# Four branches of the second block in three reduced-precision products, begun inside the last attention round

## The chip, the cores and the metric

One of the eight cores of a Trainium2 chip runs the kernel. The metric is the device time of one execution in microseconds (us), median over the executions. TensorE (PE) multiplies matrices, ScalarE (ACT) applies functions and copies, VectorE (DVE) does elementwise work, SyncE (SP) issues the transfers from HBM. TensorE writes to PSUM, which has 8 banks.

## What is computed

Two transformer blocks of width 1,024 on 256 tokens, in fp32. The first has two layers (a convolution and gating mixer with a feed-forward part, then latent attention with eight experts). The second block, which the change touches, is, cut to its mixer:

```python
h = rms_norm(x, norm_mix)
qa, ka, va, u, qm, km, vm, gates = split_in(h @ w_in)
ya = swa_attention(qa, ka, va, sinks, slopes_swa) @ w_o_swa      # 512 -> 1024
z  = gelu(s5_ssm(u, ...)) @ w_glu                                # 512 -> 1024
yb = (z[..., :512] * sigmoid(z[..., 512:])) @ w_o_ssm            # 512 -> 1024
yc = moba_attention(qm, km, vm, slopes_moba) @ w_o_moba          # 512 -> 1024
g = sigmoid(gates)
mixed = g[..., :1024] * ya + g[..., 1024:2048] * yb + g[..., 2048:] * yc
x = x + mixed @ w_out
```

and a feed-forward part (1,024 to 4,096 and back) follows. The products with w_o_swa, w_glu, w_o_moba and w_o_ssm are the four branches.

## The kernel before

Each engine has its own program, written out by hand; semaphores order them, and no scheduler moves anything. Activations lie transposed, features on the partitions and 256 tokens along the columns. Weights come from HBM in chunks of 2 MB into `ring`, which has 3 places: chunk n goes to place n % 3, and SyncE issues it once the chunk three before is used up. In the second block the chunks are numbered `C2_A`, `C2_B`, `C2_QA`, ... `C2_SWA` (10) to `C2_SSM` (13), then `C2_OUT`, `C2_FF1`, `C2_FF2`.

**Attention rounds.** A loop `for r in range(ROUNDS + 1)` with ROUNDS = 8 runs the state-space scan of round r beside the two attention heads of round r - 1, and between them TensorE does the projections that are left (24 tiles of gates). A head a goes through `scores` (TensorE, L1428 and L1429), `biased` (VectorE, L2644 on), `soft` (ScalarE, L1912), `normalised` (VectorE, L2661 to L2664), `turn2` (three transposes on TensorE, L1436), `take_turned` (ScalarE, L1922) and `values` (TensorE). There is one PSUM bank for the transposed probabilities. In the last turn, r = 8, neither scan nor projection is left: only the last output of the scan (`state_output`, its gelu on ScalarE at L1938) and heads 14 and 15. ScalarE's copy of their result (L1954) ends the round.

**Branches.** Each branch has 8 tiles of 128 output features; a tile is 4 matmuls of 256 columns (`group`, L915) in one bank, from bank g % 8. Before a tile with g of 8 or more TensorE waits until VectorE has emptied tile g - 8 (`s_br_free`). VectorE multiplies each tile by its gate and adds it to `mixed` (first branch L2685, later L2690 and L2692); for w_glu ScalarE takes the sigmoid of one tile (L1959), and VectorE multiplies it by the next (L2699). The order is w_o_swa, w_o_moba, w_glu, w_o_ssm. Then the output projection multiplies `mixed` by w_out, 8 tiles of 8 matmuls, also by `group`.

**Matmuls here.** `group` multiplies plain fp32 operands; the trace shows two records for each of its matmuls. `product` (L922 to L924) splits both operands in a high part, copied to fp32r by ScalarE, and a low part, the difference, made by VectorE, and sums high x high, high x low, low x high: three matmuls of one record each. The feed-forward part of the second block already uses `product`; a weight unit there is 128 partitions x 1,024 numbers, split by one ScalarE copy (L1961) and one VectorE subtraction (L2712).

## Time and profile before

| | us |
|---|---|
| median of 3 runs | 2283.11 |
| lowest and highest | 2281.93, 2283.22 |
| the profiled execution, its own time | 2281.74 |
| its span, first to last instruction | 2280.0 |

The profile is of one execution. Its times are counted from the span's start. Its own time is 1.74 us above the span and 1.37 us below the median of the runs. "Idle before" a row, in brackets, is how long the engine stood still ahead of it, with what ended the wait. The end of a matmul is modelled; the distance from one start to the next is what an unbroken stream of them costs. A matmul's record in a timeline can stand for many (x192), so that a row's length is that of the group.

### The profile page before, as it was taken

What the parts mean: (1) busy time and instruction counts of PE and PEld (TensorE: products, weight loads), DVE (VectorE), ACT (ScalarE), POOL (GpSimd) and SP (SyncE); (2) the same over time, 40 slices, a digit from 0 to 9 for tenths busy, and PEclk for the clock granted to TensorE, in tenths of its full rate; (3) what the DMA queues carried; (4) which work ended last, traced back from release to release, by engine and by line L of the source; (5) the groups of instructions that cost most, each with busy time, mean ns of one, the idle gap of its engine ahead of it and who ended that gap; (6) DMA issues with size and microseconds to landing.
All of it is one profiled execution on the core that took longest, in us unless ns stands there. A gap on an engine that the chain in (4) does not pass through costs nothing.

```text
span 2280.0 us, 35361 instructions
## 1 busy us (share of the span) xinstructions
PE 2141.0 (94%) x14994; PEld 1323.6 (58%) x14994; DVE 827.5 (36%) x1568; ACT 518.9 (23%) x965; POOL 56.8 (2%) x93
## 2 busy tenths in 40 slices
PE   5998899999978989998899999999999999899997
PEld 2566688888844573432323343343333878788997
DVE  4798522234532442132001200200123366525554
ACT  4124322234421421001000100000001143303443
POOL 0000000000014000000000000000002000000000
PEclk8999999999999989999989999999999999999999
DMA  9884233222212139999999999999996323144541
GB/s 375 332 349 168 75 110 106 79 101 102 85 44 111 56 136 378 362 378 404 416 413 394 375 398 384 391 361 400 412 398 233 111 76 110 74 148 167 180 174 52
DMA packets 160307, 536.69 MB, mean 235 GB/s; under 512 B 7072, under 2 KB 31776, under 8 KB 139168
## 3 DMA queue, kind: packets, MB, share of 16 engines
q1 hardware_dynamic: 160016, 534.08, 61.7%
q8 instruction: 108, 1.77, 0.3%
q0 software_dynamic: 144, 0.52, 0.1%
q14 instruction: 39, 0.32, 0.0%
HBM read 533.53 MB, written 1.05 MB: 234 GB/s over the span
## 4 chain that ended last, share of the span: by engine, by line
PE 81%; DVE 8%; DMA 6%; DVEq 3%; issue 1%; ACT 1%; SPq 0%; ACTq 0%
PE psum L915 15%; PE psum L1302 15%; PE psum L922 9%; PE psum L923 9%; PE psum L924 9%; PE psum L1306 6%; PE psum L1327 6%; DMA ring<-in_o_exp_w 4%; PE psum L1331 3%; DVE region L2160 2%; DVEq L2163 1%; PE psum L939 1%; DMA region<-in_o_exp_w 1%; PE psum L1235 1%; DVE rstd L2023 1%
## 5 line engine op out<-in xcount | busy, mean ns | idle before, releaser
L922 PE MATMUL psum<-region_r 128*128 128x512 f32 (+1 forms) x1232 | 434.6, 353 | 25.6 <-DVE region_r L2252 8.7
L923 PE MATMUL psum<-region_r 128*128 128x512 f32 (+1 forms) x1136 | 392.2, 345 | 0.0
L924 PE MATMUL psum<-region_r 128*128 128x512 f32 (+1 forms) x1136 | 390.5, 344 | 0.0
L922 PEld LDWEIGHTS psum<-region_r 128*128 128x128 f32 x1232 | 236.9, 192 | 69.7 <-issue 31.9
L924 PEld LDWEIGHTS psum<-region_r 128*128 128x128 f32 x1136 | 217.8, 192 | 25.3
L923 PEld LDWEIGHTS psum<-region_r 128*128 128x128 f32 x1136 | 218.0, 192 | 24.8
L1302 PE MATMUL psum<-ring,region 128*32 128x512 f32 (+1 forms) x1792 | 183.4, 542 | 2.3 <-DMA ring<-in_o_exp_w 2.3
L915 PE MATMUL psum<-H,ring 128*128 128x256 f32 (+1 forms) x656 | 156.3, 396 | 6.1 <-ACT H L1615 6.1
L1302 PE MATMUL psum<-region 128*32 128x512 f32 (+1 forms) x1520 | 153.3, 535 | 2.5 <-DMA region<-in_o_exp_w 1.5
L915 PE MATMUL psum<-region,ring 128*128 128x256 f32 (+1 forms) x592 | 139.1, 396 | 12.2 <-DVE region L2301 9.6
L915 PEld LDWEIGHTS psum<-H,ring 128*128 128x128 f32 x656 | 124.5, 192 | 34.5 <-issue 16.2
L915 PEld LDWEIGHTS psum<-region,ring 128*128 128x128 f32 x592 | 113.0, 192 | 38.0 <-issue 20.6
L1302 PEld LDWEIGHTS psum<-ring,region 128*32 128x32 f32 x1792 | 56.5, 110 | 112.2 <-issue 97.4
L2485 DVE COPY rstd<-psum 128x512 f32<-128x512 f32 x6 | 4.2, 692 | 292.7 <-PE psum L1331 260.8
L1831 ACT ACTIVATE region<-psum 128x256 f32<-128x256 f32 (+2 forms) x56 | 24.8, 450 | 373.7 <-PE psum L1259 280.3
L2498 DVE COPY region<-psum 64x512 f32<-64x512 f32 (+1 forms) x56 | 35.1, 626 | 186.8 <-PE psum L1306 186.1
L1302 PEld LDWEIGHTS psum<-region 128*32 128x32 f32 x1520 | 48.2, 110 | 91.1 <-issue 78.7
L1306 PE MATMUL psum<-ring,region 128*32 128x512 f32 (+1 forms) x832 | 98.4, 564 | 2.7 <-DMA ring<-in_o_exp_w 2.7
L2535 DVE TENSOR_TENSOR region<-region,psum 128x512 f32<-128x512 f32 (+1 forms) x28 | 17.0, 620 | 227.1 <-PE psum L1306 183.9
L1306 PE MATMUL psum<-region 128*32 128x512 f32 (+1 forms) x792 | 87.7, 539 | 5.0 <-DMA region<-in_o_exp_w 4.3
L1327 PE MATMUL psum<-ring,region 128*32 128x512 f32 x736 | 86.2, 594 | 2.2 <-DMA ring<-in_o_exp_w 2.2
L2160 DVE SCALAR_TENSOR_TENSOR region<-region,param 128x512 f32<-128x512 f32 x120 | 84.8, 748 | 4.1 <-issue 0.4
(362 smaller groups left out, 2452.5 us busy)
## 6 DMA issues: line engine op xcount, KB each, us to landing
ring<-in_o_exp_w SPq DMA_DIRECT2D x165, 1024.0 KB, 10.3
region<-in_o_exp_w SPq DMA_DIRECT2D x141, 1024.0 KB, 10.5
ring<-in_w_ada SPq DMA_DIRECT2D x24, 2048.0 KB, 10.3
ring<-in_w_ff SPq DMA_DIRECT2D x16, 2048.0 KB, 8.0
H<-in_o_exp_w SPq DMA_DIRECT2D x30, 1024.0 KB, 10.3
ring<-in_e_ffn_w SPq DMA_DIRECT2D x22, 1024.0 KB, 7.8
ring<-in_w_in SPq DMA_DIRECT2D x10, 2048.0 KB, 8.0
region<-in_e_w_in SPq DMA_DIRECT2D x4, 2048.0 KB, 16.0
```

The lines of the kernel that those rows point to most:

```text
L915: mm = pe.matmul(dst, lhsT, rhs, start=(i == 0), stop=(i == len(pairs) - 1))
L922: pe.matmul(out, a_hi, b_hi, start=first, stop=False)
L923: pe.matmul(out, a_hi, b_lo, start=False, stop=False)
L924: mm = pe.matmul(out, a_lo, b_hi, start=False, stop=last)
L939: mm = pe.matmul(bank(NORM_BANK.get(n, 7))[:, 0:w], ones[:, :], squares[:, tile, 0:w], start=(k == 0), stop=(k == kt - 1))
L1302: mm = pe.matmul(psum[r:r + 32, to, 0:width], x_full[:, k, slot0 + 32 * tg:slot0 + 32 * tg + 32], moving, start=(k == 0), stop=(k == KT - 1))
L1306: mm = pe.matmul(psum[r:r + 32, to, 0:width], x_full[:, k, slot0:slot0 + 32], moving, start=(k < 2), stop=(k >= KT - 2))
L1327: mm = pe.matmul(psum[r:r + 32, grp.down[q], :], he[:, i, slot0 + 32 * tg:slot0 + 32 * tg + 32], moving, start=(i == 0), stop=(i == ET - 1))
L1331: mm = pe.matmul(psum[r:r + 32, grp.down[q], :], he[:, i, slot0:slot0 + 32], moving, start=(i < 2), stop=(i >= ET - 2))
L1831: act.activation(he[:, tiles, slot0:slot0 + w].rearrange("p (b c) w -> p c b w", b=b), bank(grp.turn[p])[:, 0:b * c * w].rearrange("p (c b ...
L2160: x = dve.scalar_tensor_tensor(conv[i], apad[:, i, :, k:k + T], taps[:, i, k:k + 1], conv[i], ALU.mult, ALU.add)
L2498: dve.tensor_copy(cross_sum[0:64, to, 0:width], psum[64:128, b, 0:width])
```

## The change

The four branches are computed with `product`. Each branch is cut in four units of two tiles; ScalarE copies a unit's weights to one of four fp32r buffers (`unit_hi`), VectorE writes the difference over the weights in `ring`, and the same is done once for the 4 x 256 values of each branch (`values_high`, `values_low`; for the last branch tile by tile). w_glu moves ahead of w_o_moba, in TensorE's work and in SyncE's order of transfers. The first two units (tiles 0 to 3) and their splits stand in the last turn of the attention loop; bank numbers are shifted by 4 for it. The output projection stays a plain `group`.

The diff, cut to its core (renamed semaphores are left out: `s_weights_hi` and `s_weights_lo` are the old `s_z_hi` and `s_z_lo`, `s_values_hi` and `s_values_lo` the old `s_bo_hi` and `s_bo_lo`):

```diff
+BRANCHES = (C2_SWA, C2_GLU, C2_MOBA, C2_SSM)
+BRANCH_UNITS = 4 * len(BRANCHES)
+UNITS_BEFORE, VALUES_BEFORE = Z_GROUPS, 4
+B_SPLIT = 4
+EARLY_UNITS = 2
+def branch_bank(g):
+    return (g + 2 * EARLY_UNITS) % 8
+def branch_tiles(u):
+    b, i = divmod(u, 4)
+    return (4 + i, i) if BRANCHES[b] == C2_GLU else (2 * i, 2 * i + 1)
...
+        unit_hi = [reg_r(21504 + 1024 * i, 1024) for i in range(B_SPLIT)]
+        qa_hi, qm_hi = reg_r(25600, 4, T), reg_r(26624, 4, T)
+        u_hi, glu_hi = reg_r(12288, 4, T), reg_r(13312, 4, T)
+        qa_lo, qm_lo, u_lo, glu_lo = reg_r(6144, 4, T), reg_r(7936, 4, T), reg_r(9728, 4, T), reg_r(19968, 4, T)
+        branch_values = [(qa, qa_hi, qa_lo), (u_T, u_hi, u_lo), (qm, qm_hi, qm_lo), (glu_z, glu_hi, glu_lo)]
...
-            for n, w in ((C2_SWA, "w_o_swa_2"), (C2_MOBA, "w_o_moba_2"), (C2_GLU, "w_glu_2"), (C2_SSM, "w_o_ssm_2")):
+            for n, w in ((C2_SWA, "w_o_swa_2"), (C2_GLU, "w_glu_2"), (C2_MOBA, "w_o_moba_2"), (C2_SSM, "w_o_ssm_2")):
...
+            def branch(b, units):
+                _, hi, lo = branch_values[b]
+                for u in (4 * b + i for i in units):
+                    pe.wait_ge(s_weights_lo, UNITS_BEFORE + u + 1)
+                    w, v = branch_hi(u), branch_unit(u, ring_r)
+                    for i, tile in enumerate(branch_tiles(u)):
+                        g = 2 * u + i
+                        if g >= 8:
+                            pe.wait_ge(s_br_free, g - 7)
+                        h = int(tile >= 4) if BRANCHES[b] == C2_GLU else i
+                        for k in range(4):
+                            if u == 4 * b and i == 0:
+                                pe.wait_ge(s_values_lo, VALUES_BEFORE + 4 * b + k + 1)
+                            mm = product(bank(branch_bank(g))[:, 0:T], [(w[:, k, h, :], v[:, k, h, :], hi[:, k, :], lo[:, k, :])], k == 0, k == 3)
+                        mm.then_inc(s_br_ready, 1)
...
+                if r == ROUNDS:
+                    pe.wait_ge(s_proj_sb, len(PROJ))
+                    pe.wait_ge(s_xs_used, ROUNDS)
+                    branch(0, range(EARLY_UNITS))
...
-            pe.wait_ge(s_proj_sb, len(PROJ))
             pe.wait_ge(s_ao_sb, 8)
             pe.wait_ge(s_y_sb, 4)
-            pe.wait_ge(s_xs_used, ROUNDS)
-            branch(C2_SWA, 0, qa, range(8))
-            branch(C2_MOBA, 8, qm, range(8))
-            branch(C2_GLU, 16, u_T, (4, 0, 5, 1, 6, 2, 7, 3))
-            pe.wait_ge(s_br_free, 24)
-            branch(C2_SSM, 24, glu_z, range(8))
+            branch(0, range(EARLY_UNITS, 4))
+            for b in range(1, len(BRANCHES)):
+                branch(b, range(4))
...
+            def unit_high(u):
+                n = BRANCHES[u // 4]
+                if u % 4 == 0:
+                    act.wait_ge(w_in[n % RING], landed2(n))
+                if u == 0:
+                    act.wait_ge(s_xs_ready, ROUNDS)
+                last = u - B_SPLIT
+                if last >= 0:
+                    act.wait_ge(s_br_ready, 2 * last + 2)
+                act.activation(branch_hi(u), branch_unit(u), ACT.Copy).then_inc(s_weights_hi, 1)
+            def values_high(b):
+                v, hi, _ = branch_values[b]
+                act.activation(hi, v, ACT.Copy).then_inc(s_values_hi, 4)
...
+                    act.drain()
+                    values_high(0)
+                    for u in range(EARLY_UNITS):
+                        unit_high(u)
...
+            act.drain()
+            unit_high(EARLY_UNITS)
+            unit_high(EARLY_UNITS + 1)
+            values_high(1)
+            values_high(2)
+            for u in range(EARLY_UNITS + 2, BRANCH_UNITS):
+                unit_high(u)
+                if 6 <= u < 10:
+                    i = u - 6
+                    act.wait_ge(s_br_ready, 8 + 2 * i + 1)
+                    if i >= 2:
+                        act.wait_ge(s_br_free, 8 + 2 * (i - 1))
+                    act.activation(glu_s[:, i % 2, :], bank(branch_bank(8 + 2 * i))[:, 0:T], ACT.Sigmoid).then_inc(s_glu_sig, 1)
+                if 8 <= u < 12:
+                    act.wait_ge(s_br_free, 8 + 2 * (u - 8) + 2)
+                    act.activation(glu_hi[:, u - 8, :], glu_z[:, u - 8, :], ACT.Copy).then_inc(s_values_hi, 1)
...
+            def unit_low(u):
+                dve.wait_ge(s_weights_hi, UNITS_BEFORE + u + 1)
+                dve.tensor_tensor(branch_unit(u, ring_r), branch_unit(u), branch_hi(u).bitcast(F32), ALU.subtract).then_inc(s_weights_lo, 1)
+            def values_low(b):
+                v, hi, lo = branch_values[b]
+                dve.wait_ge(s_values_hi, VALUES_BEFORE + 4 * b + 4)
+                dve.tensor_tensor(lo, v, hi.bitcast(F32), ALU.subtract).then_inc(s_values_lo, 4)
...
+                    values_low(0)
+                    for u in range(EARLY_UNITS):
+                        unit_low(u)
...
+            unit_low(EARLY_UNITS)
+            unit_low(EARLY_UNITS + 1)
+            dve.wait_ge(s_proj_sb, len(PROJ))
+            values_low(1)
+            for u in range(BRANCH_UNITS):
+                b, i = divmod(u, 4)
+                if EARLY_UNITS + 2 <= u + 2 < BRANCH_UNITS:
+                    unit_low(u + 2)
+                if u == 4:
+                    values_low(2)
+                if b == 2:
+                    dve.wait_ge(s_values_hi, VALUES_BEFORE + 12 + i + 1)
+                    dve.tensor_tensor(glu_lo[:, i, :], glu_z[:, i, :], glu_hi[:, i, :].bitcast(F32), ALU.subtract).then_inc(s_values_lo, 1)
+                if b == 0:
+                    for g in (2 * u, 2 * u + 1):
+                        dve.wait_ge(s_br_ready, g + 1)
+                        dve.tensor_tensor(mixed[:, g, :], bank(branch_bank(g))[:, 0:T], gates[:, g, :], ALU.mult).then_inc(s_br_free, 1)
+                if b == 1:
+                    dve.wait_ge(s_glu_sig, i + 1)
+                    dve.wait_ge(s_br_ready, 8 + 2 * i + 2)
+                    dve.tensor_tensor(glu_z[:, i, :], bank(branch_bank(9 + 2 * i))[:, 0:T], glu_s[:, i % 2, :], ALU.mult).then_inc(s_br_free, 2)
+                if b >= 2:
+                    for g in (2 * u, 2 * u + 1):
+                        add_branch(g, 16 if b == 2 else 8)
```

How the rows of each engine's program move, at three places (line numbers of before are those of the profile; after the change `group` is L950, `product` L957 to L959, the scores L1463 and L1464, the transposes L1471).

TensorE at the end of the last attention round, in the kernel before; `region,ring` rows are the branches, and brackets name the semaphores that a row waits for:

```order
L1429 MATMUL psum<-region 128x256
L1436 MATMUL psum<-const,region 128x128 [waits apt_sb,ap_ready]
L1436 MATMUL psum<-const,region 128x128 x2
L1436 MATMUL psum<-const,region 128x128 [waits apt_sb,ap_ready]
L1436 MATMUL psum<-const,region 128x128 x2
L915 MATMUL psum<-region 64x128 [waits y_sb,ao_sb,apt_sb]
L915 MATMUL psum<-region 64x128 x2
L915 MATMUL psum<-region 64x128 [waits apt_sb]
L915 MATMUL psum<-region 64x128 x2
L915 MATMUL psum<-region,ring 128x256 [waits xs_used,y_sb,w_in1,ao_sb,proj_sb]
```

The same place after the change, where the semaphores of the splits go by their program names z_lo and bo_lo:

```order
L1464 MATMUL psum<-region 128x256
L957 MATMUL psum<-region_r 128x256 [waits z_lo,bo_lo,xs_used,proj_sb]
L958 MATMUL psum<-region_r 128x256
L959 MATMUL psum<-region_r,ring_r 128x256
...
L1471 MATMUL psum<-const,region 128x128 [waits apt_sb,ap_ready]
...
L950 MATMUL psum<-region 64x128 [waits apt_sb]
L950 MATMUL psum<-region 64x128 x2
L957 MATMUL psum<-region_r 128x256 [waits z_lo,y_sb,ao_sb]
```

48 matmuls of tiles 0 to 3 now stand between the last scores and the first transpose; the other 28 tiles stand behind the last values, as before.

ScalarE from the last turn of the loop on, after the change (L2017 ends a round's heads, L1980 and L1975 are copies of values and of weight units, L2001 is the gelu, L1953 the exponentials, L1963 the copy of transposed probabilities):

```order
L2017 ACTIVATE region<-psum 128x256 [waits ao_ready]
L1980 ACTIVATE region_r<-region 128x1024
L1975 ACTIVATE region_r<-ring 128x1024 [waits xs_ready,w_in1]
L1975 ACTIVATE region_r<-ring 128x1024
L2001 ACT_TABLE_LOAD
L2001 ACTIVATE region<-psum 128x256 [waits y_psum]
...
L1963 ACTIVATE region<-psum 128x384 [waits ao_ready,apt_ready] x2
L2017 ACTIVATE region<-psum 128x256 [waits ao_ready]
L1975 ACTIVATE region_r<-ring 128x1024 x2
L1980 ACTIVATE region_r<-region 128x1024 x2
L1975 ACTIVATE region_r<-ring 128x1024 [waits br_ready,w_in2]
```

Before the change the gelu and its table load followed the first of these rows at once. Three copies of 1,024 columns now stand ahead of it, and the copies of the third and fourth unit stand behind the round's last copy.

VectorE in the third branch after the change (L2743 is the subtraction for a weight unit, L2790 that for a tile of the gated values, L2774 and L2776 take a tile into `mixed`):

```order
L2743 TENSOR_TENSOR ring_r<-ring,region_r 128x4x256 [waits z_hi]
L2790 TENSOR_TENSOR region_r<-region,region_r 128x256 [waits bo_hi]
L2774 TENSOR_TENSOR region<-psum,region 128x256 [waits br_ready]
L2776 TENSOR_TENSOR region<-region 128x256
L2774 TENSOR_TENSOR region<-psum,region 128x256 [waits br_ready]
L2776 TENSOR_TENSOR region<-region 128x256
```

Before, a tile was taken into `mixed` by two rows of the same kind (L2690 and L2692), and nothing else stood there: the first two of these rows are new for every two tiles.

## Rows read from the trace of the kernel before

**Rows 1.** The page: the span, and the chain that ended last by line.

```profile
span 2280.0 us, 35361 instructions
...
PE psum L915 15%; PE psum L1302 15%; PE psum L922 9%; PE psum L923 9%; PE psum L924 9%; PE psum L1306 6%; PE psum L1327 6%; DMA ring<-in_o_exp_w 4%; PE psum L1331 3%; DVE region L2160 2%; DVEq L2163 1%; PE psum L939 1%; DMA region<-in_o_exp_w 1%; PE psum L1235 1%; DVE rstd L2023 1%
```

**Rows 2.** Timeline of TensorE, end of attention to out-projection: start, us, line, operation, count.

```profile
1966.88 0.49 PE L1436 MATMUL psum<-const,region 128*128 128x128 f32 x3
...
1973.76 0.61 PE L1429 MATMUL psum<-region 64*128 64x256 f32 x4
1978.05 0.90 PE L1436 MATMUL psum<-const,region 128*128 128x128 f32 x3 [3.68 <-DVE region L2664]
1979.62 0.87 PE L1436 MATMUL psum<-const,region 128*128 128x128 f32 x3 [0.67 <-ACT region L1922]
...
1983.13 42.38 PE L915 MATMUL psum<-region,ring 128*128 128x256 f32 x192 [0.52 <-issue]
2026.13 14.08 PE L915 MATMUL psum<-region,ring 128*128 128x256 f32 x64 [0.62 <-DVE region L2699]
2041.23 3.94 PE L915 MATMUL psum<-region,ring 128*128 128x256 f32 x17 [1.02 <-DVE region L2692]
```

**Rows 3.** Timeline of TensorE in the first feed-forward product, at either clock.

```profile
2075.59 0.41 PE L922 MATMUL psum<-region_r 128*128 128x256 f32 x1
2075.80 0.41 PE L923 MATMUL psum<-region_r 128*128 128x256 f32 x1
...
2095.23 0.28 PE L922 MATMUL psum<-region_r 128*128 128x256 f32 x1
2095.35 0.28 PE L923 MATMUL psum<-region_r 128*128 128x256 f32 x1
```

**Rows 4.** Timeline of ScalarE around the last attention round.

```profile
1968.85 0.38 ACT L1954 ACTIVATE region<-psum 128x256 f32<-128x256 f32 x1 [0.96 <-PE psum L915]
1969.26 1.28 ACT L1938 ACT_TABLE_LOAD   x1
1973.54 0.38 ACT L1938 ACTIVATE region<-psum 128x256 f32<-128x256 f32 x1 [3.00 <-PE psum L915]
```

**Rows 5.** Timeline of VectorE: last attention round, then one tile of the second branch.

```profile
1974.39 0.55 DVE L2644 SCALAR_TENSOR_TENSOR region<-const,psum 128x384 f32<-128x384 f32 x1 [6.17 <-PE psum L1429]
...
1978.80 0.35 DVE L2664 TENSOR_SCALAR region<-region,small 128x256 f32<-128x256 f32 x1
...
1999.65 0.42 DVE L2690 TENSOR_TENSOR region<-psum,region 128x256 f32<-128x256 f32 x1 [1.30 <-PE psum L915]
2000.15 0.43 DVE L2692 TENSOR_TENSOR region<-region 128x256 f32<-128x256 f32 x1
```

**Rows 6.** Groups of ScalarE by form in the feed-forward stage: us, mean ns.

```profile
L1961 ACT ACTIVATE region_r<-ring 128x1024 fp32r<-128x1024 f32 x31 | 31.2, 1060 | 0.0
```

**Rows 7.** Timeline of VectorE: a subtraction of 1,024 columns and what follows.

```profile
2076.05 1.22 DVE L2712 TENSOR_TENSOR region_r<-ring,region_r 128x1024 fp32r<-128x1024 f32 x1
2077.18 0.48 DVE L2027 SCALAR_TENSOR_TENSOR H<-X,param,rstd 128x256 f32<-128x256 f32 x1
```

**Rows 8.** Timeline of TensorE: a short gap in the first mixer.

```profile
181.01 2.52 PE L1009 MATMUL psum<-region,ones 128*128 128x512 f32 x4 [1.94 <-DVE region L2160]
```

**Rows 9.** Windows: busy us per engine, then clock, DMA share, GB/s.

```profile
182.00:183.00 1.00, 1.00 (x4) 0.50 (x2) 1.00 (x3) 0.00 (x0) 0.00 (x0) 0.66 1.05 410
...
185.00:186.00 1.00, 1.00 (x4) 0.84 (x3) 0.66 (x3) 0.96 (x3) 0.00 (x0) 0.63 0.11 41
...
1977.00:1978.00 1.00, 0.00 (x0) 0.00 (x0) 0.84 (x5) 0.67 (x3) 0.00 (x0) 0.87 0.00 0
...
1984.00:1985.00 1.00, 1.00 (x5) 0.77 (x5) 0.00 (x0) 0.34 (x1) 0.00 (x0) 0.72 0.09 16
```

**Rows 10.** DMA of the fourth branch's weights: its issue, and us to landing.

```profile
1997.92 0.37 SPq L870 DMA_DIRECT2D ring<-in_w_o_ssm  x1
...
ring<-in_w_o_ssm SPq DMA_DIRECT2D x1, 2048.0 KB, 7.8
```

More of the change, by code:

```diff
@@ L384, in build @@
         s_mh_hi = sem("mh_hi")
-        s_z_hi = sem("z_hi")
-        s_z_lo = sem("z_lo")
+        s_weights_hi = sem("z_hi")
+        s_weights_lo = sem("z_lo")
         s_heads_in = sem("heads_in")
-        s_bo_hi = sem("bo_hi")
-        s_bo_lo = sem("bo_lo")
+        s_values_hi = sem("bo_hi")
+        s_values_lo = sem("bo_lo")
         s_cat_hi = sem("cat_hi")
@@ L729, in out_lo, with branch_unit, branch_hi @@
             return out_unit(q, ring_r)
+        def branch_unit(u, memory=ring):
+            n = BRANCHES[u // 4]
+            v = memory[:, n % RING, :].rearrange("p (k n) -> p k n", k=4)
+            if n == C2_GLU:
+                return v.rearrange("p k (h c) -> p k h c", h=2)[:, :, :, P * (u % 4):P * (u % 4) + P]
+            return v[:, :, 2 * P * (u % 4):2 * P * (u % 4) + 2 * P].rearrange("p k (h c) -> p k h c", h=2)
+        def branch_hi(u):
+            return unit_hi[u % B_SPLIT].rearrange("p (k h c) -> p k h c", k=4, h=2)
         def cols(w, c, n, rows=None):
@@ L1032, in _ @@
                 if q < 2:
-                    pe.wait_ge(s_bo_lo, 2 * kk + 2)
+                    pe.wait_ge(s_values_lo, 2 * kk + 2)
                 if q == 2:
@@ L1484, in _ @@
                     values(2 * r - 1)
-            def branch(n, first, src, order):
-                pe.wait_ge(w_in[n % RING], landed2(n))
-                w = slot(n, 4, D)
-                for i, tile in enumerate(order):
-                    g = first + i
-                    if g >= 8:
-                        pe.wait_ge(s_br_free, g - 7)
-                    group(bank(g % 8)[:, 0:T], [(w[:, k, tile * P:(tile + 1) * P], src[:, k, :]) for k in range(4)]
-                          ).then_inc(s_br_ready, 1)
-            pe.wait_ge(s_proj_sb, len(PROJ))
             pe.wait_ge(s_ao_sb, 8)
             pe.wait_ge(s_y_sb, 4)
-            pe.wait_ge(s_xs_used, ROUNDS)
-            branch(C2_SWA, 0, qa, range(8))
-            branch(C2_MOBA, 8, qm, range(8))
-            branch(C2_GLU, 16, u_T, (4, 0, 5, 1, 6, 2, 7, 3))
-            pe.wait_ge(s_br_free, 24)
-            branch(C2_SSM, 24, glu_z, range(8))
+            branch(0, range(EARLY_UNITS, 4))
+            for b in range(1, len(BRANCHES)):
+                branch(b, range(4))
             pe.wait_ge(s_br_free, 32)
@@ L1653, in weights_hi @@
                     act.wait_ge(s_z_ready, m - 1)
-                act.activation(z_hi(m), z_unit(m), ACT.Copy).then_inc(s_z_hi, 1)
+                act.activation(z_hi(m), z_unit(m), ACT.Copy).then_inc(s_weights_hi, 1)
             weights_hi(0)
@@ L1701, in _ @@
                 act.wait_ge(s_bo_ready, i + 1)
-                act.activation(cat_hi[:, 4 + i, :], u_out[:, i, :], ACT.Copy).then_inc(s_bo_hi, 1)
+                act.activation(cat_hi[:, 4 + i, :], u_out[:, i, :], ACT.Copy).then_inc(s_values_hi, 1)
             act.wait_ge(s_lna_sum, 2)
@@ L1954, in _ @@
                     act.activation(dst[:, (r - 1) % 4, :], bank(3)[:, 0:T], ACT.Copy).then_inc(s_ao_sb, 1)
-            for i in range(4):
-                act.wait_ge(s_br_ready, 16 + 2 * i + 1)
-                if i >= 2:
-                    act.wait_ge(s_br_free, 16 + 2 * (i - 1))
-                act.activation(glu_s[:, i % 2, :], bank((16 + 2 * i) % 8)[:, 0:T], ACT.Sigmoid).then_inc(s_glu_sig, 1)
+            act.drain()
[14 more added lines that the diff above has]
+                    act.activation(glu_hi[:, u - 8, :], glu_z[:, u - 8, :], ACT.Copy).then_inc(s_values_hi, 1)
             def ff1_split(cs, u):
@@ L2669, in _ @@
                     state_drive(r)
+                else:
+                    values_low(0)
+                    for u in range(EARLY_UNITS):
+                        unit_low(u)
                 if r:
@@ L2679, in _ @@
                     state_scan(r, 1)
-            dve.wait_ge(s_proj_sb, len(PROJ))
-            for g in range(8):
-                dve.wait_ge(s_br_ready, g + 1)
-                dve.tensor_tensor(mixed[:, g, :], bank(g)[:, 0:T], gates[:, g, :], ALU.mult).then_inc(s_br_free, 1)
             def add_branch(g, gate0):
```

24 lines of the change are left out of this document (9 added, 15 removed).

## The prediction

> **What bounds the kernel now.** I read the page first, then the timeline of TensorE over the part that changes. By the page TensorE's plain matmuls at L915 hold 15% of the chain that ended last, and the waiting there is small [rows 1]: whatever is saved in TensorE's stream in the branches comes off the end, as long as nothing else takes its place. The timeline shows that stream [rows 2]. After the last scores, whose end is 1974.37, TensorE stands still for 3.68 us until VectorE has normalised head 14, then does the two turns and the values at a slow pace, and begins the branches at 1983.13. They run without a break but for 0.62 us ahead of the fourth (w_glu's last product), and the output projection starts at 2041.23. So the stretch to be changed is 58.1 us, and the 8.8 us before it are mostly waiting. All other stages keep their instructions.
>
> **What a tile costs.** Before: the 64 records of the fourth branch stand for 8 tiles of 4 matmuls and last 14.08 us, less a modelled tail of about 0.3: 13.8 / 8 = 1.73 us a tile, 0.43 a matmul [rows 2]. After: 12 matmuls of `product`. The same form in the feed-forward part, 256 columns, starts every 0.12 us at full clock and every 0.21 at half clock [rows 3], so 1.44 us a tile or 2.55. That is 0.29 us less a tile at full clock.
>
> The FP8 and Floating Point Precision page of the Trainium skill (TensorE Precision Notes) says that true fp32 takes four passes through the array, of which `product` makes three. By the page a tile would fall by a quarter, to 1.30 us, and 28 tiles would save 12.0 us where the rows give 8.1. The 0.12 us of the rows decides the sum: the page's version stands below as a rival.
>
> **The last round.** ScalarE ends the seventh round's heads at 1968.85 + 0.38 = 1969.23 [rows 4]. New there: one copy of values and two of weight units, 1.06 us each by the feed-forward rows [rows 6], so until about 1972.4. The gelu's table load (1.28 us) followed at 1969.26 and now follows at 1972.4; it ends at 1973.7, while the gelu began at 1973.54 when TensorE had finished its input [rows 4]. That is 0.15 us late, and nothing waits for it so soon. VectorE was idle for 6.17 us before 1974.39 [rows 5]. Its three subtractions take 1.13 us each from start to start [rows 7], the first one behind ScalarE's first copy at 1970.4: they end at about 1974.0, 0.4 ahead of the softmax work of head 14. So both engines hide their early splits, and units 0 and 1 are ready when TensorE has sent off the scores at 1974.3. Without this cover each microsecond would still be free up to about 1 us, since the softmax ends (1978.80 + 0.35 = 1979.15 [rows 5]) before TensorE is through with the early tiles.
>
> TensorE then runs 48 matmuls x 0.12 = 5.76 us, to 1980.1. The idle 3.68 us are filled and 2.05 us are pushed behind. First turn to second turn took 1.57 us at half clock [rows 2]; at full clock, with a copy of about 0.5 us between them, I take 1.1: the second turn at 1981.2. In round seven, at full clock, ScalarE's closing copy began 1.97 us after the second turn (1966.88 to 1968.85 [rows 2, 4]) and took 0.38: 1983.55.
>
> **The new wait.** Only behind that copy does ScalarE begin with unit 2, and VectorE subtracts only when the copy is made: 0.1 + 1.06 + 1.22 + 0.05 = 2.4 us [rows 6, 7]. TensorE has nothing else queued behind it and stands still from about 1983.15 to 1986.0. That is 2.9 us later than the branches started before, with 28 tiles to go instead of 32.
>
> **The rest of the branches.** 28 x 1.44 = 40.3 us, to 2026.3. Can the splits keep up? A unit is 2.88 us of TensorE. ScalarE has 1.06 us a unit and at most 0.8 more. VectorE has 1.13, plus 0.84 in the first branch and 0.42 in the second; in the third 1.13 + 0.42 for the gated values + 2 x 0.93 (0.50 from multiply to add, then 0.43 [rows 5]) = 3.41, half a microsecond over. It lags, but it subtracts two units ahead. I followed it through: counted from the start of the third branch its last low part of gated values is there at 12.3 us, and TensorE wants it at 4 x 2.88 + 3 x 0.36 = 12.6. So nothing waits, by 0.3 us. If each of its four waits a unit costs 0.1 us more, 1.6 us over the branch, TensorE stands for up to 1.3 us: the upper end of this cost, 0 the lower, and I take 0. The fourth branch needs only 2.99 a unit, and no weights for its last two. The 0.62 us of wait between w_glu and w_o_ssm goes, as the third branch lies between them now. Weights: w_o_ssm is issued when the first branch is done, about 1992 instead of 1997.92, lands 7.8 us later [rows 10] and is copied after 2006; the others land as early, counted from their use. Four PSUM banks lie between a tile and its emptying, as before.
>
> **The clock.** After an idle stretch TensorE is granted half its clock. Here it fell at 1977.7 and rose at 1984.6 (worked out from 0.87 and 0.72 as the means of these two windows [rows 9]), so before the change the end of the round and 1.4 us of the branches ran slow. A gap of just 1.94 us, until 181.01, was followed by a fall at 182.3, and the clock came back at 185.7 [rows 8, 9]. With its early tiles TensorE keeps its clock through the turns, but the new gap of 2.9 us is longer than that one, so I expect a fall about when unit 2 begins. The two slow stretches lasted 3.4 and 6.8 us; a microsecond of them loses 1 - 0.12 / 0.213 = 0.44 us. That is 1.5 us for the short one, about 2.5 for the long one without what of it lies in the gap (3.0 with it), 0 if the clock stays: I take 1.8.
>
> The page TensorE: Matmul & The Clock Gate of the Trainium skill (Why this matters for your kernels) advises against gaps between bursts of matmuls for this reason. [...]
>
> **The sum.** 2026.3 + 0.16 (modelled tail) + 1.02 (the same wait for the last tile of `mixed` [rows 2]) + 1.8 = 2029.3 instead of 2041.2: 11.9 us less. Made up of 8.1 for 28 cheaper tiles, 6.9 for four tiles gone from the stretch, 0.6 for the wait, 0.6 for slow clock at the old start, less 2.9 and 1.8; the remainder is rounding. The profiled execution took 2281.74, so it gives 2269.8. That execution lies 1.4 under the median of the runs, 2283.11, from which it gives 2271.2; I forecast 2270.8. A change of 0.2% (4.6 us) is about what this measurement can tell.
>
> **The rivals.**
> - *The clock stays up*: no fall follows the gap. For it: in both stretches the fall came 3.3 us after the idle time began (at 1974.37 and about 179.07), and here work is back after 2.9. Against it: so it was in the second stretch, after 1.94. 13.7 us less, 2269.0 (15%).
> - *Clock and splits both worse*: the long slow stretch, and VectorE up to 1.3 us late in the third branch. 9.5 us less, 2273.5 (8%).
> - *Three quarters of a plain tile*: a matmul of `product` at a quarter of the plain one's 0.43 us, 0.108, which saves 3.9 us more in 28 tiles and 0.6 in the early ones. 2266.3. Against it: 0.12 in the feed-forward part [rows 3] (2%). This is the rule of the Trainium skill's FP8 and Floating Point Precision page cited above.
> - *It does not act*: weights or values late by so much that the saving is eaten, within 4.6 us of before. Needs 7.3 us of new waits, half a microsecond a unit; no row shows that (2%).
> - *Slower*: the split chain goes in step with TensorE. If a unit's copy and subtraction (2.4 us with their waits) came behind the unit before it instead of beside it, 14 units would cost 33 us: 2304. It decides from 0.85 us of wait a unit, where the 11.9 us are gone. Against it: four buffers for the high parts, and units are subtracted two ahead (3%).
>
> The likeliest case, 70%, has 2269 to 2273 as its own range. The range for 8 in 10 is 2267.5 to 2274.5, which takes in the first two rivals and the 1.4 us between profile and runs. Faster by over 0.2%: 95%. Within 0.2%: 2%. Slower: 3%.
>
> **What would show it.** In the profile after: 48 `product` matmuls from about 1974.3, without a gap before the first turn at 1980.1; a gap of 2.5 to 3.3 us ahead of unit 2, released by VectorE's subtraction; the granted clock 1.0 until then and half for 3 to 6 us after; matmuls 0.12 us apart from there to about 2028; no wait of over 0.3 us in the third and fourth branch. It is wrong if matmuls with low weights in `ring` stand further apart, if the clock stays low, or if VectorE releases TensorE again and again.

## The result and the profile after

| | before | after |
|---|---|---|
| median of 5 runs, us | 2281.93 | 2267.50 |
| lowest and highest | 2280.16, 2283.22 | 2262.80, 2271.60 |
| the profiled execution, its own time | 2281.74 | 2262.80 |
| its span | 2280.0 | 2261.0 |

The ratio is 0.9934 [0.9920, 0.9948], so 12 to 18 us faster; the forecast had 95% on faster. The forecast of 2270.8 was reckoned from a median of 2283.11 over 3 runs; over 5 runs the median of before is 2281.93, 1.2 us lower. From median to median the change gave 14.4 us where 12.3 were forecast. The page of the changed kernel, span and chain, answers to [rows 1]:

```profile
span 2261.0 us, 35681 instructions
...
PE psum L1337 15%; PE psum L950 12%; PE psum L957 10%; PE psum L958 10%; PE psum L959 10%; PE psum L1341 7%; PE psum L1362 6%; DMA ring<-in_o_exp_w 4%; PE psum L1366 3%; DVE region L2234 2%; DVEq L2237 1%; PE psum L974 1%; DMA region<-in_o_exp_w 1%; PE psum L1270 1%; DVE rstd L2097 1%
```

The 15% that the plain matmuls of `group` held are now split: L950 (`group`) 12%, and 10% for each line of `product`, where the branches join the feed-forward part.

TensorE's timeline over the stretch that changed, which answers to [rows 2]:

```profile
1968.33 0.61 PE L1464 MATMUL psum<-region 64*128 64x256 f32 x4
1968.87 0.38 PE L957 MATMUL psum<-region_r 128*128 128x256 f32 x1
...
1974.54 0.28 PE L959 MATMUL psum<-region_r,ring_r 128*128 128x256 f32 x1
1974.66 0.49 PE L1471 MATMUL psum<-const,region 128*128 128x128 f32 x3
1975.83 0.52 PE L1471 MATMUL psum<-const,region 128*128 128x128 f32 x3 [0.67 <-ACT region L1963]
1976.27 1.52 PE L950 MATMUL psum<-region 128*64 128x128 f32 x12
1980.76 0.36 PE L957 MATMUL psum<-region_r 128*128 128x256 f32 x1 [2.96 <-DVE ring_r L2743]
...
1989.83 0.28 PE L958 MATMUL psum<-region_r 128*128 128x256 f32 x1
1989.95 0.28 PE L959 MATMUL psum<-region_r,ring_r 128*128 128x256 f32 x1
...
2020.47 0.28 PE L959 MATMUL psum<-region_r,ring_r 128*128 128x256 f32 x1
2022.12 2.21 PE L950 MATMUL psum<-region,ring 128*128 128x256 f32 x9 [1.37 <-DVE region L2776]
```

Behind the scores 48 matmuls of `product` follow without a break, then the first turn at 1974.66 and the second 1.17 us later. Behind head 15's values TensorE waits 2.96 us, and VectorE's subtraction of a weight unit (L2743) ends it. From 1980.76 on it never waits until the output projection, ahead of which it stands 1.37 us for the last tile of `mixed`.

Two things lie in the 19.0 us between the spans. I take two marks. The first is ScalarE's copy that ends the heads of round seven; up to it the engines run the same instructions in both programs; only the transfers of w_glu and w_o_moba, 2 MB each, come in exchanged order. The second is VectorE's first update of X behind the output projection. "The stretch" below is the time from the first mark to the second. ScalarE's timeline of after, for the first mark and for [rows 4]:

```profile
1963.43 0.38 ACT L2017 ACTIVATE region<-psum 128x256 f32<-128x256 f32 x1 [0.96 <-PE psum L950]
1963.89 1.06 ACT L1980 ACTIVATE region_r<-region 128x1024 fp32r<-128x1024 f32 x1
1964.85 1.99 ACT L1975 ACTIVATE region_r<-ring 128x1024 fp32r<-128x1024 f32 x2
1966.86 1.28 ACT L2001 ACT_TABLE_LOAD   x1
1968.15 0.38 ACT L2001 ACTIVATE region<-psum 128x256 f32<-128x256 f32 x1
...
1977.83 0.38 ACT L2017 ACTIVATE region<-psum 128x256 f32<-128x256 f32 x1 [0.96 <-PE psum L950]
1978.30 2.00 ACT L1975 ACTIVATE region_r<-ring 128x1024 fp32r<-128x1024 f32 x2
```

And VectorE's, which answers to [rows 5] and holds the second mark:

```profile
1966.19 2.35 DVE L2743 TENSOR_TENSOR ring_r<-ring,region_r 128x1024 fp32r<-128x1024 f32 x2
1968.96 0.55 DVE L2718 SCALAR_TENSOR_TENSOR region<-const,psum 128x384 f32<-128x384 f32 x1 [0.42 <-PE psum L1464]
...
1979.38 2.36 DVE L2743 TENSOR_TENSOR ring_r<-ring,region_r 128x1024 fp32r<-128x1024 f32 x2 [5.66 <-ACT region_r L1975]
...
2001.76 1.22 DVE L2743 TENSOR_TENSOR ring_r<-ring,region_r 128x1024 fp32r<-128x1024 f32 x1
...
2004.90 1.22 DVE L2743 TENSOR_TENSOR ring_r<-ring,region_r 128x1024 fp32r<-128x1024 f32 x1
...
2020.79 0.42 DVE L2774 TENSOR_TENSOR region<-psum,region 128x256 f32<-128x256 f32 x1 [0.49 <-PE psum L959]
2021.64 0.42 DVE L2776 TENSOR_TENSOR region<-region 128x256 f32<-128x256 f32 x1 [0.43 <-issue]
2025.88 0.42 DVE L2805 TENSOR_TENSOR X<-X,psum 128x256 f32<-128x256 f32 x1 [3.81 <-PE psum L950]
```

The second mark in the profile of before:

```profile
2044.99 0.42 DVE L2705 TENSOR_TENSOR X<-X,psum 128x256 f32<-128x256 f32 x1 [3.81 <-PE psum L915]
```

The first mark stands at 1963.43, and in the profile of before at 1968.85 [rows 4]: 5.4 us ahead of the change. The first two experiments show that profiles of one and the same kernel differ there by as much. From mark to mark it was 76.14 us before and is 62.45 now: in these two profiles **13.7 us lie where the change is**. Behind the second mark both take 235 us.

| in the stretch | before | forecast | after |
|---|---|---|---|
| first mark to the end of the scores | 5.5 | 5.5 | 5.4 |
| early tiles | - | 5.8 | 5.8 |
| from there to the branches or unit 2 | 8.8 | 5.9 | 6.1 |
| branches, to the output projection | 58.1 | 43.3 | 41.4 |
| to the second mark | 3.8 | 3.8 | 3.8 |

The forecast's 43.3 are 40.3 + 0.16 + 1.02 + 1.8. Its last summand, 1.8 us for a fall of the clock, is where it is off: this profile has nothing of it. The windows of after (busy us of PE, PEld, DVE, ACT, POOL, then granted clock, DMA share, GB/s) have no fall behind the gap, against [rows 9]:

```profile
1980.00:1981.00 1.00, 0.24 (x2) 0.27 (x3) 1.00 (x2) 1.00 (x2) 0.00 (x0) 1.00 0.00 0
1981.00:1982.00 1.00, 1.00 (x10) 1.00 (x10) 1.00 (x2) 1.00 (x2) 0.00 (x0) 1.00 0.00 0
```

### The profile page after: what moved, and what is told of

It reads as the page before. It is cut to its first block, busy times and chain, and to the rows that moved or that the text cites. A ratio compares the mean times of both kernels' runs of the same rounds, so it can differ in the third digit from the quotient of the medians.

```text
span 2261.0 us, 35681 instructions
## 1 busy us (share of the span) xinstructions
PE 2122.1 (94%) x15122; PEld 1317.5 (58%) x15122; DVE 848.6 (38%) x1591; ACT 539.2 (24%) x988; POOL 56.9 (3%) x93
## 4 chain that ended last, share of the span: by engine, by line
PE 81%; DVE 7%; DMA 7%; DVEq 3%; issue 1%; ACT 1%; SPq 0%; ACTq 0%
PE psum L1337 15%; PE psum L950 12%; PE psum L957 10%; PE psum L958 10%; PE psum L959 10%; PE psum L1341 7%; PE psum L1362 6%; DMA ring<-in_o_exp_w 4%; PE psum L1366 3%; DVE region L2234 2%; DVEq L2237 1%; PE psum L974 1%; DMA region<-in_o_exp_w 1%; PE psum L1270 1%; DVE rstd L2097 1%
## 5 line engine op out<-in xcount | busy, mean ns | idle before, releaser
L957 PE MATMUL psum<-region_r 128*128 128x512 f32 (+1 forms) x1360 | 469.6, 345 | 29.5 <-DVE region_r L2326 8.8
L958 PE MATMUL psum<-region_r 128*128 128x512 f32 (+1 forms) x1264 | 427.3, 338 | 0.0
L959 PE MATMUL psum<-region_r 128*128 128x512 f32 (+1 forms) x1136 | 390.3, 344 | 0.0
L957 PEld LDWEIGHTS psum<-region_r 128*128 128x128 f32 x1360 | 260.2, 191 | 74.0 <-issue 36.3
L958 PEld LDWEIGHTS psum<-region_r 128*128 128x128 f32 x1264 | 242.2, 192 | 24.7
L959 PEld LDWEIGHTS psum<-region_r 128*128 128x128 f32 x1136 | 217.7, 192 | 25.0
L950 PE MATMUL psum<-H,ring 128*128 128x256 f32 (+1 forms) x656 | 156.2, 396 | 6.1 <-ACT H L1656 6.1
L950 PEld LDWEIGHTS psum<-H,ring 128*128 128x128 f32 x656 | 124.4, 192 | 34.4 <-issue 16.2
L950 PE MATMUL psum<-region,ring 128*128 128x256 f32 (+1 forms) x336 | 82.6, 406 | 11.4 <-DVE region L2375 9.6
L1362 PE MATMUL psum<-region 128*32 128x512 f32 x688 | 83.4, 614 | 2.8 <-issue 1.6
```

The lines of the kernel that those rows point to most:

```text
L950: mm = pe.matmul(dst, lhsT, rhs, start=(i == 0), stop=(i == len(pairs) - 1))
L957: pe.matmul(out, a_hi, b_hi, start=first, stop=False)
L958: pe.matmul(out, a_hi, b_lo, start=False, stop=False)
L959: mm = pe.matmul(out, a_lo, b_hi, start=False, stop=last)
L1362: mm = pe.matmul(psum[r:r + 32, grp.down[q], :], he[:, i, slot0 + 32 * tg:slot0 + 32 * tg + 32], moving, start=(i == 0), stop=(i == ET - 1))
```

## The experiments

Each gives the stretch from its profile, which leaves out what scatters ahead of the first mark, and the ratio to the kernel before where it was run more than once. "Slow clock" is the time of the stretch at half clock, summed over windows of 1 us as (1 - granted clock) x 2. Each stretch is of one profile, and in the changed kernel the clock alone moves it by up to 2.6 us.

### The kernel before, once more

No edit. It asks what the clock and the stretch of one and the same kernel do from one execution to the next.

> The kernel before, once more, as a kernel of its own. In the two profiles so far the last attention round's closing copy stands at 1968.85 (before) and 1963.43 us (after), though nothing ahead of it was changed. Theory A, chance from one execution to the next: this profile's copy stands anywhere within 1962 to 1970 us, the times of the runs spread over some 3 to 9 us, and the ratio to before is 1.000 within 0.002. Rival B, the changed kernel really runs 5 us faster ahead of the branches: this profile's copy stands within 1 us of 1968.85. From there to the start of the output projection it takes 72.4 us by both.

Median 2280.50 against 2280.76, ratio 1.000 [0.999, 1.001]. In its profile the first mark stands at 1966.84, 2.0 us earlier than in the first profile of the same kernel. The stretch is 78.06, 1.9 longer, with 10.24 us of slow clock instead of 6.82. Its timeline and windows:

```profile
1980.76 44.67 PE L915 MATMUL psum<-region,ring 128*128 128x256 f32 x192 [0.52 <-issue]
...
2041.14 4.15 PE L915 MATMUL psum<-region,ring 128*128 128x256 f32 x18 [1.02 <-DVE region L2692]
```

```profile
1976.00:1977.00 1.00, 0.55 (x3) 0.31 (x3) 0.59 (x3) 0.69 (x3) 0.00 (x0) 0.79 0.00 0
...
1986.00:1987.00 1.00, 1.00 (x4) 0.82 (x3) 0.00 (x0) 0.00 (x0) 0.00 (x0) 0.59 0.00 0
```

The fall is already there at 1976 and lasts past 1986. Two profiles of one kernel so differ by 2.0 us ahead of the stretch and by 1.9 in it. The mark lies where theory A puts it and not where B does. The 72.4 us that both expected up to the output projection were 74.3, longer by the same 1.9, and the times spread over 9.6 us instead of at most 9. In the largest set of executions of before, 17 of them, the times reach from 2276.92 to 2287.12.

### The changed kernel, in three more profiles

No edit in any of the three; only the first was timed over several executions.

> The changed kernel once more, for a second sample of TensorE's clock at the gap ahead of unit 2 (in its first profile the gap was 2.96 us and the clock stayed at full speed, where a fall and a loss of 1.8 us had been forecast) and of its time. Theory A, it is chance whether the clock falls there: the stretch from round seven's closing copy to the first update of X is 62.45 us as before if it stays, 64 to 65.5 us if it falls. Rival B, the clock never falls at this gap: 62.45 within 0.2 us. The ratio to before is 0.9934 within 0.0015 by both.

> The changed kernel, a third look at TensorE's clock at its gap of 2.96 us ahead of unit 2. Theory A, chance with a fall at least every second time: of this look and the next at least one shows a fall and a stretch of 64 to 65.5 us. Rival B, a gap of this length here does not bring the clock down, or seldom: both show full clock and 62.4 us.

> The changed kernel, a fourth look, as the one before it: at least one fall in the two by theory A, none by rival B.

The median of the first is 2269.25 (2263.98 to 2269.48) against 2280.57, ratio 0.9944 [0.9931, 0.9957]. The other two took 2273.76 and 2271.05. The stretch was 62.44, 65.09 and 65.08, with a gap of 2.96 us ahead of unit 2 in all of them. The first kept its clock, and the other two lost it, so theory A holds in all three. The second of the three, its timeline and its windows:

```profile
1987.90 0.55 PE L957 MATMUL psum<-region_r 128*128 128x256 f32 x1 [2.96 <-DVE ring_r L2743]
...
1988.46 0.41 PE L959 MATMUL psum<-region_r,ring_r 128*128 128x256 f32 x1
1988.67 0.41 PE L957 MATMUL psum<-region_r 128*128 128x256 f32 x1
```

```profile
1987.00:1988.00 1.00, 0.10 (x1) 0.13 (x1) 1.00 (x2) 1.00 (x2) 0.00 (x0) 0.51 0.00 0
...
1993.00:1994.00 1.00, 1.00 (x7) 1.00 (x7) 0.61 (x2) 0.61 (x1) 0.00 (x0) 0.58 0.00 0
```

Matmuls start 0.21 us apart, the pace of half clock in [rows 3], from the first behind the gap on; the clock is back at 1993.8. That is 6.82 us of slow clock, of which 0.9 lie in the gap, and 2.64 us more of stretch. So the same gap costs 0 or 2.64 us, 2 of 4 each; the mean is 1.3. The first marks of the four profiles of the changed kernel stand at 1963.43, 1964.78, 1967.90 and 1970.58, so 7.2 us apart in one kernel: the 5.4 us ahead of the change are no more than that.

### No early tiles

```diff
-EARLY_UNITS = 2
+EARLY_UNITS = 0
```

All 32 tiles by `product`, all behind the last values.

> The changed kernel with no unit begun in the last attention round: all 16 units behind it. Theory A: the idle time ahead of the first turn comes back (3.7 us), the clock falls there, and the first unit waits for its split behind the round's end (3 us). Against the changed kernel 5.76 us of matmuls come back into the stretch, less the 2.1 us by which they had pushed the turns, plus 2 to 3 us of slow clock: 5 to 7 us more than the changed kernel, so 7 to 9 less than before. Rival B, the early units are worth nothing, since the turns wait for them: within 1 us of the changed kernel.

2273.87 (2272.38 to 2275.91), ratio 0.9965 [0.9951, 0.9979]; stretch 70.43. The chain of waits, with the total, the count and the longest in us:

```profile
PE psum L1471 <- DVE region L2738: 3.9, 1, 3.9
PE psum L957 <- DVE ring_r L2743: 3.1, 1, 3.1
```

The wait for head 14's softmax (L2738) is back, the gap for the splits stays, and the clock is slow for 13.64 us. From profile to profile `product` and the new order give 5.7 us of stretch without early tiles (76.14 to 70.43). The early tiles are worth another 8.0 against the profile of the changed kernel that kept its clock, above the 5 to 7 that A expected, and 6.7 against the mean of its four profiles (63.8). The slow clock is part of it; how much of the 13.64 us is due to the missing early tiles, and how much to the gap of 3.1 us, this one profile doesn't show.

### The early tiles alone, plain

The kernel before, with tiles 0 to 3 of w_o_swa as plain `group` behind the last scores and the banks shifted; old order of the branches.

```diff
+                if r == ROUNDS:
+                    pe.wait_ge(s_proj_sb, len(PROJ))
+                    pe.wait_ge(s_xs_used, ROUNDS)
+                    branch(C2_SWA, 0, qa, range(4))
...
-            branch(C2_SWA, 0, qa, range(8))
+            branch(C2_SWA, 4, qa, range(4, 8))
```

> The kernel before with tiles 0 to 3 of the first branch, as plain matmuls, begun behind the last scores; no splits, the old order of branches. Theory A: 4 x 1.73 = 6.9 us of matmuls fill the 3.68 us of idle time and push the turns by 3.2 us; the clock stays up in the turns and at the start of the branches, which is worth 1.5 to 2.5 us. The stretch gets 6.9 - 3.2 + 2 = 5 to 6 us shorter, so about two fifths of the change's gain comes from the place alone, without any cheaper matmul. Rival B, the gain of the change is that of the cheaper matmuls: under 2 us less than before.

2274.89 (2272.48 to 2277.58), ratio 0.9974 [0.9962, 0.9985]; stretch 70.33, clock full throughout. TensorE:

```profile
1969.32 7.17 PE L915 MATMUL psum<-region,ring 128*128 128x256 f32 x32
1976.33 0.49 PE L1436 MATMUL psum<-const,region 128*128 128x128 f32 x3
...
1979.93 34.80 PE L915 MATMUL psum<-region,ring 128*128 128x256 f32 x160 [0.47 <-ACT region L1956]
2015.35 14.08 PE L915 MATMUL psum<-region,ring 128*128 128x256 f32 x64 [0.61 <-DVE region L2701]
2030.45 4.80 PE L915 MATMUL psum<-region,ring 128*128 128x256 f32 x21 [1.02 <-DVE region L2694]
```

This is 5.8 us less than before, within A's 5 to 6 and as much as `product` without early tiles. From here to the whole change, in the profile that kept its clock, it is 7.9 us. The four early tiles take 5.79 us instead of 7.01, the other 28 take 39.99 instead of 48.89 (50.52 less the waits of 0.61 and 1.02), together 10.1; the wait of 0.61 goes; the gap costs 2.5 (2.96 against 0.47), and the last wait 0.35. That makes 7.9.

### The gap lengthened

```diff
             act.drain()
-            unit_high(EARLY_UNITS)
-            unit_high(EARLY_UNITS + 1)
             values_high(1)
             values_high(2)
+            unit_high(EARLY_UNITS)
+            unit_high(EARLY_UNITS + 1)
```

> The changed kernel with ScalarE's two copies of values (1.9 us) ahead of its copies of units 2 and 3 instead of behind them, so that the gap ahead of unit 2 grows from 2.96 to 4.9 us. Theory A, the clock falls after a gap of this length for certain: the stretch grows by 1.9 us for the wait and 1.5 to 2.5 us for the slow clock, to 65.8 to 66.9. Rival B, only the wait counts: 64.4 us and no window under full clock. Rival C, the lead of the splits gives it back: under 63.5.

2271.15 (2267.04 to 2273.69), ratio 0.9954 [0.9940, 0.9967]. The gap is 4.85 us, the clock falls for 3.42 us, and the stretch is 65.86: 1.9 for the gap and 1.5 for the clock. The fall begins at 1987.7, 0.4 us behind the end of the gap, and is over at 1991.1. A's range of 65.8 to 66.9 us holds:

```profile
1987.00:1988.00 1.00, 0.71 (x5) 0.74 (x6) 1.00 (x2) 1.00 (x2) 0.00 (x0) 0.85 0.00 0
...
1991.00:1992.00 1.00, 1.00 (x10) 1.00 (x10) 1.00 (x2) 0.07 (x1) 0.00 (x0) 0.94 0.00 0
```

### A gap between the two, in two profiles

Only `values_high(1)` goes ahead of the two units; both profiles are of the same code.

> The changed kernel with one of ScalarE's two copies of values ahead of those of units 2 and 3, so that the gap ahead of unit 2 is about 3.9 us, between the 2.96 at which no fall was seen in two profiles and the 4.85 at which one was. Stretch 63.4 us if only the wait counts, 64.9 or more if the clock falls. Theory A, chance: either. Rival B, a fall comes once the gap is long enough: if it falls here, it should in both looks.

> The same kernel as the look before, to tell chance from a fixed length: by rival B both looks show the same, by theory A they can differ.

2271.57 and 2270.10, the gap 3.91 us in both, the stretch 65.60 and 65.82, slow clock 6.82 in both. The fall comes inside the gap:

```profile
1982.00:1983.00 1.00, 0.00 (x0) 0.00 (x0) 0.00 (x0) 1.00 (x2) 0.00 (x0) 0.92 0.03 8
...
1989.00:1990.00 1.00, 1.00 (x8) 1.00 (x8) 0.68 (x2) 0.00 (x0) 0.00 (x0) 0.67 0.00 0
```

With 4.85 us above and 4.09 in the last experiment, each of the four gaps of 3.9 us or more ahead of unit 2 had a fall. Both profiles show one, as rival B expects, but two that agree don't rule out theory A. The stretch is 3.3 longer than 62.45 in the mean, 0.95 of it for the gap and 2.3 for the clock.

### The splits of units 2 and 3 ahead of the turns

```diff
+                if r == ROUNDS:
+                    unit_high(EARLY_UNITS)
+                    unit_high(EARLY_UNITS + 1)
                 if r:
                     take_turned(2 * r - 2)
...
             act.drain()
-            unit_high(EARLY_UNITS)
-            unit_high(EARLY_UNITS + 1)
```

> The changed kernel with ScalarE's copies of weight units 2 and 3 moved ahead of its two copies of turned probabilities (it idles 2.29 us there), so that VectorE subtracts them before the values are done. Theory A, the gap of 2.96 us ahead of unit 2 is the split chain alone: it shrinks to about 0.6 us (the wait for the round's closing copy), the stretch from the closing copy of round seven to the output projection falls from 58.6 to about 56.2 us, and the time is 2.4 us less than that of the changed kernel. Rival B, the copies delay the turns: the first copy of turned probabilities starts up to 0.5 us later and half of the gain is lost. Rival C, another wait takes the gap's place (VectorE busy with subtractions while tiles 0 to 3 wait for it): the gap stays above 1.5 us.

2264.06 (2261.78 to 2268.87), ratio 0.9920 [0.9906, 0.9933]; stretch 59.99, at full clock. ScalarE there:

```profile
1980.09 2.00 ACT L1975 ACTIVATE region_r<-ring 128x1024 fp32r<-128x1024 f32 x2
1982.46 0.49 ACT L1963 ACTIVATE region<-psum 128x384 f32<-128x384 f32 x1 [0.38 <-PE psum L1471]
```

The two copies lie between the softmax and the first copy of turned probabilities, which still waits 0.38 us for TensorE, so B's delay did not come. The gap is 0.47 us, left by ScalarE's closing copy alone:

```profile
1985.54 0.39 PE L957 MATMUL psum<-region_r 128*128 128x256 f32 x1 [0.47 <-ACT region L2020]
```

So the gap of the change came from ScalarE's order, and with it goes 2.46 us of the stretch.

### The same, with the closing wait ahead of the first branch's last tile

```diff
+                        if g == 7:
+                            pe.wait_ge(s_ao_sb, 8)
+                            pe.wait_ge(s_y_sb, 4)
...
-            pe.wait_ge(s_ao_sb, 8)
-            pe.wait_ge(s_y_sb, 4)
             branch(0, range(EARLY_UNITS, 4))
```

> As e2 (copies of units 2 and 3 ahead of the copies of turned probabilities), and TensorE's wait for the round's closing copy and the gelu stands ahead of tile 7, the first whose bank the attention still used, instead of ahead of unit 2. Theory A: the last 0.47 us of wait between the values and unit 2 goes, the stretch is 59.5 us instead of 59.99 and 62.45, the time 2.9 us less than the changed kernel. Rival B, the wait shows up at the end instead, since VectorE is late with the last tiles: stretch 60.0 as in e2.

2263.84 (2263.08 to 2265.06), ratio 0.9923 [0.9910, 0.9936]; stretch 59.44, no gap at all. This is the shortest stretch of all, 3.0 us under the change and 16.7 under before. This is theory A's 59.5. The times of the last two versions can't be told apart. Both have a shorter stretch and a lower median than the changed kernel in either of its measurements, though the intervals of the ratios overlap; all five executions of this one were at 2265.06 or less, and 3 of the twelve of the changed kernel.

### VectorE loaded

```diff
                 dve.wait_ge(s_weights_hi, UNITS_BEFORE + u + 1)
+                if u >= EARLY_UNITS:
+                    dve.reduce_max(sm(384 + u, 1), unit_hi[u % B_SPLIT].bitcast(F32), AX)
```

A reduction ahead of each subtraction, whose result nothing uses: 1.13 us more of VectorE a unit.

> The changed kernel with one more VectorE instruction ahead of each of the 14 subtractions behind the attention: the maximum over the unit's 1,024 high parts, about 1.1 us, written where nobody reads. It measures how much cover VectorE has in the branches. Theory A, VectorE is almost as full as TensorE there (it idles under 5 of its 42 us in the changed kernel's profile): the 15.4 us of new work come out for the most part, 9 to 12 us more in the stretch. Rival B, the lead of two units hides it: under 3 us more. If A holds, an addition of 0.85 us a unit would be enough to lose most of the change's gain.

2278.23 (2275.29 to 2284.75), ratio 0.9991 [0.9981, 1.0001]; stretch 73.30. TensorE's waits:

```profile
PE psum L957 <- DVE ring_r L2745: 5.7, 3, 4.1
PE psum L957 <- DVE region_r L2792: 3.3, 1, 3.3
```

5.7 us in three waits for weights (4.09 is the gap itself, longer by the one reduction ahead of unit 2's subtraction; 0.41 and 1.16 are in the third branch) and 3.3 for gated values at the start of the fourth, so 6.0 us more than the 2.96 of the change. The clock is slow for 13.66 us in two falls, one inside the first gap and one inside the wait of 3.3 us; 9.4 of them lie outside the waits and cost some 4.2 us by the 0.44 of the other runs. The last wait is 0.4 shorter, and 1.1 of the 10.85 us have no cause that these rows show. The sum is within theory A's 9 to 12 us, but its reason holds in part only: of 15.8 us of new work (14 x 1.13) 6.0 came out as waits, and the clock added most of the rest. 1.13 us more a unit on VectorE takes nearly all of the gain. So the margin in the third branch is small.

## Why the prediction was right in its splits, waits and pace, and wrong in its clock

- **The early splits are hidden: right.** ScalarE's three copies run from 1963.89 to 1966.8, the gelu at 1968.15 waits for nothing new, and VectorE's subtractions end 0.42 us ahead of the softmax work (its idle time at 1968.96).
- **48 early matmuls, 5.76 us, no gap: right**, 5.79.
- **The turns and the new gap: right.** Second turn 1.17 us after the first (1.1), closing copy 2.00 after it (1.97), gap 2.96 ("2.5 to 3.3"), released by VectorE's subtraction. The reordered copies showed its cause.
- **28 cheaper tiles, 8.1 us: right in kind, 0.5 short.** 39.99 less a tail of 0.16 is 39.83, by 336 matmuls 0.1185 us and not 0.12. The FP8 and Floating Point Precision page of the Trainium skill (TensorE Precision Notes) counts four passes for true fp32, by which one would be a quarter of the plain matmul's 0.43 [rows 2], an estimate of 0.108. The trace does not agree, with 0.1185: only 0.5 us of the 3.9 that this rival added came.
- **VectorE keeps up in the third branch: right.** Its units stand 3.14 us apart (2001.76 to 2004.90), and not the 3.41 of the forecast, and no wait of TensorE shows; a further 1.13 us a unit did bring waits.
- **Waits: right but for 0.35 us.** The one ahead of w_o_ssm is gone; the last one is 1.37 us instead of 1.02. The 0.35 lie on VectorE: the addition of the last tile starts 0.85 us after its multiplication (2020.79 and 2021.64), where it was 0.50 [rows 5]. The profile names no cause.
- **The clock: this step failed.** "I expect a fall" rested mainly on a single event, a fall after a gap of 1.94 us, and charged 1.8 us. In the first profile of the changed kernel there was none, and over four profiles the cost was 0, 0, 2.64 and 2.64. The gap's length alone doesn't decide it: one program, with 2.96 us each time, did both. The rival "the clock stays up" at 15% should have had about half. It gave 13.7 us less, which is what this profile shows, in part by luck: two smaller misses, + 0.5 and - 0.35, nearly cancel. The price of a fall was right. The prediction took 0.44 us for each microsecond of slow clock and 2.5 for the long fall, and the falls ahead of unit 2 cost 0.44 to 0.45 for each one outside the gap.
- **The range: too narrow, by the same step.** It treated the profile of before as exact. Two profiles of before differ by 1.9 us in the stretch, since the slow clock there lasted 6.82 and 10.24 us, and equal code ahead of the stretch by several more. The mean of both profiles of before is 77.1 and that of four of the changed kernel 63.8: 13.3 us less.

From profile to profile the sum closes: 11.9 forecast, + 1.8 for the clock, + 0.5 for the pace, - 0.35 for the last wait is 13.8, and 13.7 were measured. The median of the five runs, 2267.50, lies 3.3 us under the forecast, at the edge of the range. Of these, 1.2 are the lower median of before, and 1.4 (13.3 - 11.9) to 1.8 (13.7 - 11.9) are in the stretch. The rest is within what executions of one program scatter: the twelve executions of the changed kernel lie between 2262.8 and 2273.8, with a median of 2269.3, and the second measurement's ratio is 0.9944. Had that one been the first, the same forecast would have been 1.6 us off.

The scatter ahead of the first mark goes with the clock only in part. Over windows of 10 us up to the mark, the clock was slow for about 109 us in the profile of before and 93 in that of after, the least of all 14, which also has the earliest mark. But the latest mark, 1970.70 in the first version with reordered splits, goes with 95 us. The cause stays open.

Two slips in the prediction's sums change nothing of this. Its list of parts adds up to 11.5 us, and the 0.4 us over are more than rounding. And its second rival, 2.4 us above the forecast by its own 9.5, would be at 2273.2 and not at 2273.5.

## What to carry to other kernels

Cut a profile at marks between which the two programs differ, and take differences there: of 19.0 us between the spans only 13.7 lay where the change is. Where work is moved into an idle stretch, look at what an in-order engine does right behind it: here a copy that was queued behind the round's last one made a new gap of 2.96 us, and moving two copies forward gave 2.46 us of it back. Here a clock fall after a gap of 2.96 us was a matter of chance, so it belongs into the range with both prices, not into the sum as one.

## What the runs showed of the hardware

- TensorE's clock falls after the same gap in some executions and not in others. Over the 13 profiles with the 1.94 us gap of [rows 8] in the first mixer (1.95 in some) it fell in 4; in the fourteenth that gap was 3.10, with a fall; behind 2.96 us in 2 of 4; behind 3.91, 3.91, 4.09 and 4.85 in each. So the one fall of [rows 8, 9] was the rarer case. The profile of after, in which it did not fall, by TensorE's timeline and by its windows:

```profile
178.97 1.98 PE L1044 MATMUL psum<-region,ones 128*128 128x512 f32 x4 [1.94 <-DVE region L2234]
```

```profile
181.00:182.00 1.00, 1.00 (x6) 0.80 (x5) 1.00 (x2) 0.00 (x0) 0.00 (x0) 1.00 1.04 406
182.00:183.00 1.00, 1.00 (x6) 0.82 (x5) 0.53 (x5) 0.01 (x1) 0.00 (x0) 1.00 0.54 207
```

- The page TensorE: Matmul & The Clock Gate of the Trainium skill (Why this matters for your kernels) advises against idle gaps between bursts of matmuls that are longer than about the change's own, 2.96 us. For gaps clearly longer the traces agree: all 81 gaps of 3.36 to 7 us that began at full clock, in the 14 profiles together, had a fall inside them or in the 4 us behind them. For shorter ones they don't: 4 of 13 gaps of 1.94 had a fall, so that the fall of [rows 8, 9] went beyond what the page says. Between the two it is a matter of the execution: for the gap of 2.96 the price was 0 or 2.64 us, and a gap of 3.29 us in the first mixer (at about 205 us) had a fall in 8 of the 14 profiles.
- A fall costs by what of it lies outside the gap, 0.44 to 0.45 us for each microsecond. With the gap of 2.96, 6.82 us of slow clock, 0.9 of them in the gap, cost 2.64. With the gap of 3.91 the same 6.82, 1.9 and 1.4 of them in the gap, cost 2.2 and 2.4. Behind the gap of 4.85, 3.42 us, all outside it, cost 1.5.
- Executions of equal code drift apart: the first mark, up to which the engines run the same instructions in all kernels here, lay between 1963.43 and 1970.70 in 14 profiles.
